# Down projection of a transformer-like layer: sixteen k-pairs instead of fifteen in seven products, one subtraction for two weight pieces, and a second weight sum fetched from DRAM

## What is computed

```python
h = rms_norm(x, attn_norm)
p = h @ w_in                                   # 2048 -> 5376 columns
mix = concat(sliding_window_attention(...), hgrn2(...))
x = x + mix @ w_out                            # 2048 x 2048
h = rms_norm(x, ffn_norm)
u = causal_conv3(h @ w_ffn_up) + conv_b        # 2048 x 11264
a, b = split(u)
x = x + (silu(a) * b) @ w_ffn_down             # 5632 x 2048
```

## Time and profile before

| | value |
|---|---|
| median of three runs | 1081.53 us |
| span of the profiled execution, first to last instruction | 1079.9 us |
| TensorE busy | 1075.4 us, 100% |
| VectorE busy | 909.8 us, 84% |
| ScalarE busy | 630.3 us, 58% |
| GpSimd busy | 70.9 us, 7% |
| data moved by DMA | 249.08 MB, mean 231 GB/s |
| mean granted TensorE clock | 0.999 of full |

### The profile page before, as it was taken

One profiled execution on the slowest core, in us unless ns is written; L12 is line 12 of the kernel. 1 busy time (PEld: TensorE's weight loads), 2 busy tenths in 40 slices (PEclk: granted clock), 3 DMA queues, 4 the chain that ended last, 5 costly groups with the idle time before them and its releaser, 6 DMA issues.

```text
span 1079.9 us, 18178 instructions
## 1 busy us (share of the span) xinstructions
PE 1075.4 (100%) x6549; PEld 930.3 (86%) x6549; DVE 909.8 (84%) x1374; ACT 630.3 (58%) x926; POOL 70.9 (7%) x100
## 2 busy tenths in 40 slices
PE   9999999999999999999999999999999999999998
PEld 9888888888888888888888888888888888888887
DVE  7878988889655678888888888888877899999997
ACT  7677676756544655555555555545555566646663
POOL 4500000000000000000000000000000000000000
PEclk9999999999999999999999999999999999999999
DMA  8654677777787978888887878788887877887882
GB/s 273 184 157 147 201 199 237 183 243 199 229 234 257 267 212 242 228 240 212 252 226 227 244 212 255 220 238 237 252 231 223 239 250 270 284 276 254 287 313 94
DMA packets 185086, 249.08 MB, mean 231 GB/s; under 512 B 9141, under 2 KB 143174, under 8 KB 184774
## 3 DMA queue, kind: packets, MB, share of 16 engines
q1 hardware_dynamic: 170134, 212.30, 61.0%
q0 software_dynamic: 12480, 31.46, 15.1%
q10 hardware_dynamic: 2416, 4.60, 1.2%
HBM read 243.75 MB, written 36.04 MB: 259 GB/s over the span
## 4 chain that ended last, share of the span: by engine, by line
PE 99%; DMA 0%; DVE 0%; issue 0%; DVEq 0%
PE bank L1791 38%; PE bank L1799 20%; PE bank L2186 7%; PE bank L2185 7%; PE bank L2184 7%; PE bank L2037 3%; PE bank L1838 3%; PE bank L2039 3%; PE bank L1840 3%; PE bank L1839 3%; PE bank L2038 3%; PE bank L1759 1%; PE bank L1867 1%; PE bank L2076 0%; DMA xt<-in_x_dram 0%; PE bank L1956 0%
## 5 line engine op out<-in xcount | busy, mean ns | idle before, releaser
L764 ACT CAST w_hi<-raw 128x1024 fp32r<-128x1024 f32 x299 | 312.2, 1049 | 255.2 <-PE bank L1799 121.9
L1173 DVE TENSOR_TENSOR w_lo<-raw,w_hi 128x1024 fp32r<-128x1024 f32 x299 | 364.2, 1223 | 110.4 <-ACT w_hi L764 109.8
L1791 PE MATMUL bank<-hs,w_hi 128*128 128x512 f32 x1792 | 423.0, 391 | 0.0
L1791 PEld LDWEIGHTS bank<-hs,w_hi 128*128 128x128 f32 x1792 | 331.2, 188 | 66.3 <-issue 0.9
L1799 PEld LDWEIGHTS bank<-hs,w_lo 128*128 128x128 f32 x1792 | 224.5, 191 | 5.7 <-issue 0.2
L1799 PE MATMUL bank<-hs,w_lo 128*128 128x256 f32 x1792 | 227.3, 283 | 0.0
L1143 ACT CAST hi_slot<-slot 128x1024 fp32r<-128x1024 f32 (+1 forms) x96 | 111.0, 1187 | 68.1 <-DVE slot L1716 33.3
L1700 DVE TENSOR_TENSOR slot_lo<-slot,hi_slot 128x1024 fp32r<-128x1024 f32 (+1 forms) x96 | 128.7, 1387 | 4.7 <-ACT hi_slot L1143 3.7
L2186 PE MATMUL bank<-hi_slot,gated 128*128 128x512 f32 (+1 forms) x202 | 78.2, 387 | 0.0
L2184 PE MATMUL bank<-hi_slot,gated 128*128 128x512 f32 (+1 forms) x202 | 78.2, 387 | 0.0
L1618 DVE SCALAR_TENSOR_TENSOR C<-U,cols,C 128x256 f32<-128x256 f32 x176 | 73.3, 479 | 0.0
(11 more groups left out here) (247 smaller groups left out, 1176.7 us busy)
## 6 DMA issues: line engine op xcount, KB each, us to landing
raw<-in_w_ffn_up_dram SPq DMA_DIRECT2D x176, 512.0 KB, 4.8
u_sums<-in_w_ffn_down_dram POOLq DMA_DIRECT2D x60, 512.0 KB, 6.9
raw<-in_w_in_dram SPq DMA_DIRECT2D x51, 512.0 KB, 4.6
slot<-in_w_ffn_down_dram SPq DMA_DIRECT2D x36, 512.0 KB, 5.0
raw<-in_w_in_dram SPq DMA_DIRECT2D x66, 256.0 KB, 3.3
raw<-in_w_out_dram SPq DMA_DIRECT2D x32, 512.0 KB, 5.2
slot<-u_sums SPq DMA_DIRECT2D x60, 256.0 KB, 5.5
slot<-in_w_ffn_down_dram SPq DMA_DIRECT2D x30, 256.0 KB, 4.0
```

Of the source, the lines that this page charges most:

```text
L764: act.copy(w_hi[:, i, :], raw[:, i, :]).then_inc(units_hi, 1)
L1173: dve.tensor_tensor(w_lo[:, i, :], raw[:, i, :], w_hi[:, i, :].bitcast(F32), ALU.subtract)\
L1791: m = pe.matmul(banks[b][:, :], w_hi[:, i, c], hs[:, 4 * i + k, :], start=(first and k == 0), stop=(final and k == 3))
```

## The change

PATTERNS gets 16 S in each string. SEVENS, the number of S in one string, follows and becomes 16, the k-pairs with parked activation sums become two, and there are fewer D. For six k-pairs (numbers 2, 4, 6, 8, 10, 12) POOL also makes t2 in DRAM, with one more copy and one more accumulating transfer, and SP loads it as block 0 of piece c; the other ten still get t2 from DVE. For each S, DVE now makes t2 (where it isn't loaded) and t4 first, then the low part of a, and then the low parts of b and c in one operation of five blocks (`split_both`). The steps of POOL start at unit 20 and are 3.5 units apart. Three of four quarters of x2 are now fetched at the later position.

```diff
-PATTERNS = ["CCCCSSSSSDSSSSSDSSSSSc", "CcSSDSSSSSDSSSSSDSSSCc"]
+PATTERNS = ["CCCCSSSSSSSSDSSSSSSSSc", "CcSSSDSSSSSSSDSSSSSSCc"]
+SECOND_SUM_IN_DRAM = (2, 4, 6, 8, 10, 12)
-SUM_STEP = (13, 3)
+FIRST_SUM_QUAD = Q_F0
+SUM_STEP = (7, 2)
-        X2_BACK_AT = [[5, 5, 17, 17], [13, 13, 19, 19]]
+        X2_BACK_AT = [[5, 17, 17, 17], [13, 19, 19, 19]]
 # wait_for_slot
-                    wait_until_used(sp, LAST_OLD - 3 if piece == "a" else LAST_OLD - 1)
+                    wait_until_used(sp, LAST_OLD - {"a": 3, "b": 1, "c": 0}[piece])
 # load_seven
+                if second_sum_in_dram(q):
+                    wait_for_slot(q, "c")
+                    sp.dma_start(raw_of(q, "c")[:, 0, :], u_sums_v[n, 2, :, pair, :])\
+                        .then_inc(second_sum_loaded[SLOT_OF[q]], 16)
-            sp.wait_ge(sums_added, 16 * 2 * SEVENS)
+            sp.wait_ge(sums_added, 16 * (2 * SEVENS + len(SECOND_SUM_IN_DRAM)))
 # gpsimd
-                pool.wait_ge(units_used, (Q_F0 + 3) * RING + step * SUM_STEP[0] // SUM_STEP[1] + RING)
+                pool.wait_ge(units_used, FIRST_SUM_QUAD * RING + step * SUM_STEP[0] // SUM_STEP[1] + RING)
+            step, copied, added = 0, 0, 0
             for n in range(SEVENS):
...
+                if n in SECOND_SUM_IN_DRAM:
+                    wait_for_step(step)
+                    pool.dma_start(u_sums_v[n, 2], column_block(2 * n + 1, 0)).then_inc(sums_copied, 16)
+                    step, copied = step + 1, copied + 1
...
+                if n in SECOND_SUM_IN_DRAM:
+                    wait_for_step(step)
+                    pool.wait_ge(sums_added, 16 * added)
+                    pool.dma_start(u_sums_v[n, 2], u_sums_v[n, 0], accum_op=ALU.add, max_dma_last_dim=2 * GT * 4).then_inc(sums_added, 16)
+                    step, added = step + 1, added + 1
 # sums_of_weights
                 wait_for_down(dve, q, "b")
-                before = raw_piece_before(q, "c")
...
-                dve.tensor_tensor(t2, t1, b21, ALU.add).then_inc(t2_made, 1)
-                dve.wait_ge(t2_made, s + 1)
+                if second_sum_in_dram(q):
+                    dve.wait_ge(second_sum_loaded[SLOT_OF[q]], second_sums_loaded(q))
+                else:
...
+                    dve.tensor_tensor(t2, t1, b21, ALU.add).then_inc(t2_made, 1)
+                    dve.wait_ge(t2_made, second_sums_made(q))
                 dve.tensor_tensor(t4, t2, b22, ALU.add).then_inc(t4_made, 1)
+            def split_both(q):
+                dve.wait_ge(units_hi, piece_number(q, "c") + 1)
+                blocks = slice(blocks_of(q, "b").start, blocks_of(q, "c").stop)
+                raw_b_and_c, lo_b_and_c = [slots[SLOT_OF[q]][as_lo][:, blocks, :] for as_lo in range(2)]
+                dve.tensor_tensor(lo_b_and_c, raw_b_and_c, hi_slots[q % HI_SLOTS][:, blocks, :].bitcast(F32),
+                                  ALU.subtract).then_inc(units_split, 2)
 # lo_of
+                if is_seven(pair, at):
+                    sums_of_weights(pair, at)
+                    split(q, "a")
+                    dve.wait_ge(t4_made, seven_of(pair, at) + 1)
+                    split_both(q)
+                    return
```

More of the change, by code:

```diff
@@ L292, in hybrid_layer @@
         partial = sb_blocks("partial", 39, 1)[:, 0, :]
-        u_sums = nc.dram_tensor("u_sums", (SEVENS * 2 * P, 2 * GT), F32)
-        u_sums_v = u_sums.ap().rearrange("(n j p) (c m) -> n j p c m", j=2, p=P, m=GT)
+        u_sums = nc.dram_tensor("u_sums", (SEVENS * 3 * P, 2 * GT), F32)
+        u_sums_v = u_sums.ap().rearrange("(n j p) (c m) -> n j p c m", j=3, p=P, m=GT)
         parked = nc.dram_tensor("x2_parked", (SEQ, D_MODEL), F32)
@@ L363, in hybrid_layer @@
         down_loaded = {piece: [sem(f"down_loaded_{piece}{n}") for n in range(SLOTS)] for piece in "ab"}
+        second_sum_loaded = [sem(f"second_sum_loaded{n}") for n in range(SMALL_SLOT)]
         four_loaded = {piece: [sem(f"four_loaded_{piece}{n}") for n in range(SMALL_SLOT)] for piece in "ab"}
@@ L426, in seven_of, with second_sum_in_dram, second_sums_loaded, second_sums_made @@
             return pair * SEVENS + SEVEN_AT[pair].index(at)
+        def second_sum_in_dram(q):
+            pair, at = divmod(q, QUADRUPLES)
+            return is_seven(pair, at) and K_PAIR_AT[pair][at] in SECOND_SUM_IN_DRAM
+        def second_sums_loaded(q):
+            n = sum(second_sum_in_dram(m) and SLOT_OF[m] == SLOT_OF[q] for m in range(OLD_RING, q + 1))
+            return 16 * n
+        def second_sums_made(q):
+            return sum(is_seven(*divmod(m, QUADRUPLES)) and not second_sum_in_dram(m) for m in range(q + 1))
         def pieces_of(q):
@@ L733, in wait_for_step @@
             def wait_for_step(step):
-                pool.wait_ge(units_used, (Q_F0 + 3) * RING + step * SUM_STEP[0] // SUM_STEP[1] + RING)
+                pool.wait_ge(units_used, FIRST_SUM_QUAD * RING + step * SUM_STEP[0] // SUM_STEP[1] + RING)
             def column_block(tile, c):
                 return w_down_v[:, tile, :].rearrange("p (pair c m) -> p pair c m", c=2, m=GT)[:, :, c, :]
+            step, copied, added = 0, 0, 0
             for n in range(SEVENS):
-                wait_for_step(4 * n)
+                wait_for_step(step)
                 pool.dma_start(u_sums_v[n, 0], column_block(2 * n, 1)).then_inc(sums_copied, 16)
-                wait_for_step(4 * n + 1)
+                wait_for_step(step + 1)
                 pool.dma_start(u_sums_v[n, 1], column_block(2 * n + 1, 0)).then_inc(sums_copied, 16)
-                wait_for_step(4 * n + 2)
-                pool.wait_ge(sums_copied, 16 * 2 * (n + 1))
+                step, copied = step + 2, copied + 2
+                if n in SECOND_SUM_IN_DRAM:
+                    wait_for_step(step)
+                    pool.dma_start(u_sums_v[n, 2], column_block(2 * n + 1, 0)).then_inc(sums_copied, 16)
+                    step, copied = step + 1, copied + 1
+                wait_for_step(step)
+                pool.wait_ge(sums_copied, 16 * copied)
                 for j in range(2):
-                    wait_for_step(4 * n + 2 + j)
+                    wait_for_step(step + j)
                     pool.dma_start(u_sums_v[n, j], column_block(2 * n, 0), accum_op=ALU.add).then_inc(sums_added, 16)
+                step, added = step + 2, added + 2
+                if n in SECOND_SUM_IN_DRAM:
+                    wait_for_step(step)
+                    pool.wait_ge(sums_added, 16 * added)
+                    pool.dma_start(u_sums_v[n, 2], u_sums_v[n, 0], accum_op=ALU.add, max_dma_last_dim=2 * GT * 4).then_inc(sums_added, 16)
+                    step, added = step + 1, added + 1
         @block.scalar
@@ L1708, in sums_of_weights @@
                 wait_for_down(dve, q, "b")
-                before = raw_piece_before(q, "c")
[L1710 to L1713, removed]
-                dve.tensor_tensor(t2, t1, b21, ALU.add).then_inc(t2_made, 1)
-                dve.wait_ge(t2_made, s + 1)
-                dve.tensor_tensor(t4, t2, b22, ALU.add).then_inc(t4_made, 1)
+                if second_sum_in_dram(q):
+                    dve.wait_ge(second_sum_loaded[SLOT_OF[q]], second_sums_loaded(q))
+                else:
+                    before = raw_piece_before(q, "c")
+                    if before is not None:
+                        wait_until_used(dve, before)
+                    elif SLOT_OF[q] == 2:
+                        wait_until_used(dve, LAST_OLD)
+                    dve.tensor_tensor(t2, t1, b21, ALU.add).then_inc(t2_made, 1)
+                    dve.wait_ge(t2_made, second_sums_made(q))
+                dve.tensor_tensor(t4, t2, b22, ALU.add).then_inc(t4_made, 1)
+            def split_both(q):
[4 more added lines that the diff above has]
+                                  ALU.subtract).then_inc(units_split, 2)
             def lo_of(pair, at):
                 q = q_of(pair, at)
+                if is_seven(pair, at):
[4 more added lines that the diff above has]
+                    return
                 for piece in pieces_of(q):
-                    if piece == "b" and is_seven(pair, at):
-                        sums_of_weights(pair, at)
-                        dve.wait_ge(t4_made, seven_of(pair, at) + 1)
                     split(q, piece)
```

## The result

The changed kernel takes 1085.90 us (median of five runs, 1085.41 to 1087.22), the kernel before 1081.54 beside it. The ratio is 1.0042, 95% interval [1.0031, 1.0052]: slower by 0.4%, 4.4 us, clear of the noise. I had forecast 1082.2 with a range to 1085.0 and had given slower a chance of 0.26.

The account below looks back on a forecast made before the run. The prediction took the matmul count as the bound while VectorE, ScalarE and loads stay ahead. -1.36 for fewer matmuls and +2.0 for stalls gave +0.6 us, a median of 1082.2, range 1080.0 to 1085.0.

Parts of the forecast that it names:

- The product count: In down, two k-pairs go from 24 to 21 matmuls, all on the path: -1.36 us.
- The mechanism: In down, VectorE's lead at piece b shrinks through runs of S until PE stalls there: +2.0 us.
- the ledger: Count of VectorE's lead at piece b, S by S through down's runs; stalls summed to +2.0 us.
- load ceiling: In down, piece b's load starts only when b of q-3 is used, capping the lead at about 0.8 to 1.1 us.
- at about the same time: In down, t2's load was to land with b's, sparing VectorE 0.71 us and raising the load ceiling some 0.4.
- the lead: Time from the end of a low part to the first matmul reading it; PE counts as stalled under 0.2 us.
- My bound for a bad landing: Loads in down landing after 6.7 us would put the load ceiling at -0.4 and stalls at about 5 us.
- The joint operation gains VectorE 0.05: One subtraction for b and c in down costs VectorE 2.76 us instead of 2.81 for each S.
- a ceiling only: In down, the high part of c waits for a free slot, capping the lead at 1.95 us, 2.6 after a D.
- Rival 1: VectorE and the loads keep up in down: stalls under 1.0, 1080.2 to 1081.1 us; chance 0.23, 0.08 for fixed part saved.
- Rival 2: Loads in down land after 6.5 us and more instead of 5.5, stalling PE: 1084 to 1086.5 us; chance 0.22.
- Rival 3: DRAM sums delay the weights of the up stage, with gaps before down: 1084 us or more; chance 0.03.

Follow-up runs that it names:

- x9_apart_k5: x1_apart with t2 of k-pair 5 instead of 6 from DRAM and the loads of x2 spread; 1080.04 us, ratio 0.9987.
- x1_apart: The changed kernel with the low parts of b and c made by two subtractions again, in the old order (a, t2, t4, b, c); 1080.66 us, ratio 0.9993.
- x10: The changed kernel with the joint subtraction, but the low part of a made ahead of t2 and t4, as before; 1111.97 us, ratio 1.0282.
- x7: The changed kernel with t2 from DRAM for all 16 k-pairs and POOL's steps 14/5 units apart; 1084.41 us, ratio 1.0038.
- x8: x1_apart with the loads of x2 spread, t2 from DRAM for all 16 k-pairs and POOL's steps 14/5 units apart; 1081.45 us, ratio 1.0006.
- x4_joint_alone: The kernel before with only the joint subtraction of b and c and its order (t2, t4, a, b+c); 1083.53 us, ratio 1.0020.
- x5_apart_more: x1_apart with t2 of a seventh k-pair from DRAM, POOL's steps 10/3 units apart and the loads of x2 spread; 1081.17 us, ratio 0.9999.

## Why the prediction was wrong

- **The product count** was right: -1.36, and x9_apart_k5 has all of it.
- **The mechanism** was right: PE stops at piece b at the ends of the runs and behind late loads, for the joint subtraction. x1_apart shows it. Its size was off: 6.3 lost in down where the ledger had 2.0.
- **The step that failed is the ledger, in its load ceiling and in a term that it lacked.**
  - *The load ceiling* was taken as 0.9, and 1.3 where t2 is loaded. For t2 I had the second sum land "at about the same time" as b's, and so a ceiling 0.4 higher; it landed 0.6 to 0.7 later, which leaves 0.1. And I took 5.2 to 5.5 for every landing. At q = 8 (b's sum after 6.1) the lead was 0.04 and not 1.05, and with it q = 8 to 11 lost 1.8 in place of 0.9. At q = 18 and 26 (7.3 and 7.2) the ceiling was under zero, and they lost 2.7 in place of 0.1. My bound for a bad landing, 6.7, was only the longest of the rows that I had picked: in the same trace of the kernel before, b's sum landed 7.6 after its issue at 892.44, and 8.4 after that at 1035.40.
  - *The restart* was not in the ledger: 0.14 for each of eleven stops, 1.5 in all, most of which is also in the sums just given. In the kernel before PE doesn't stop in down, so its rows there could not show it.
  - At q = 32 and 41 the lead was used up where I had 0.2 and 0.5 left. For q = 32 the leads behind the D had begun 0.1 lower, and an S cost VectorE 5.37 where I had 5.34. For q = 41 it was the second sum once more: VectorE waited 0.74 for it at q = 40.
- **"The joint operation gains VectorE 0.05"** was half right. The next operation starts 2.74 after it (901.68 and 904.42), where the two took 2.81: a gain of 0.07. But an S cost 5.37 (the operations start at 901.68 and 907.05), against 5.39, since the joint one starts only when c's high part is there. That it must wait for that part stood in the prediction as a ceiling only, and x10 shows that it is the stronger bond.
- **Rival 1**, the whole fixed part saved, fell: the fixed part of the Trainium skill ("VectorE: DVE Perf Modes", errata section) is there in the length, 2.826 for 2560 elements, but what a merge saves is in the distances, 0.07.
- **Rival 2**, loads that land later, was part of the truth. Its reason was the traffic of the second sums, with landings of 6.5 and more in place of 5.5; the median went to 5.6. But single late loads, which the kernel before has too, met a lead that the joint operation had used up. More traffic with less work for VectorE (x7 against the changed kernel) was faster, not slower. The point at which it decides, a load ceiling under 0.2, was met at q = 8, 18 and 26.
- **Rival 3**, sums that delay an earlier stage, did not show in the change, where down begins no later than before, and did in x7 and x8.
- **The range** ended at 1085.0, in the middle of rival 2's times; its upper bound of 1086.5 would have held 1085.9.
- **Left open**: what the slower executions of x4_joint_alone (up to 1084.8) and x5_apart_more (up to 1083.0) lose, which no trace caught. The kernels whose lead comes near zero spread by 1 to 3 us, x7 by 6, and x10, which stalls all along, by 0.1; the kernel before by up to 0.6. Why single loads land 2 us later than the median stays open too, beyond the loads of x2 ahead of q = 18.

## What to carry to other kernels

Where a pipeline runs with a lead, keep a ledger of the lead at each hand-over, and work it out once more with the worst value of each term in the whole trace, not only with the median: at q = 18 and 26 two late loads cost 2.7 of the 6.3. A load that is to relieve an engine must itself land before the engine needs it. Joining two operations makes the first result as late as the second and makes the joint one wait for the inputs of both; it pays only where the lead can spare that, or where the fixed cost seen in the distance between starts (0.07 here) is worth more. Spend relief where the lead is smallest, at the end of a run, and not behind a refill, where a ceiling takes it away.

## What the runs showed of the hardware

- A stop of TensorE costs more than its length. The first matmul starts 0.05 after the end of what it waited for, and the second follows 0.33 to 0.34 after the first instead of 0.23, at each of the eleven stops of the changed kernel; with the distances behind it a restart costs 0.14, the granted clock at 1.00.
- The view of waits gave 3.3 us for PE in down where the distances between starts gave 6.3: the ends of matmuls in it are modelled, and a restart is no wait.
- A load of 256 KB issued from SP in down landed after 3.1 to 9.0 us, in one execution of the changed kernel (issued at 925.83 and 861.38).
